# A two-layer hybrid decoder trunk on one core: six column sums per layer, each as two streamed passes over a rounded part and its rest

## The reference

```python
def rms_norm(x, g, eps=NORM_EPS):
    y = x * lax.rsqrt(jnp.mean(x * x, axis=-1, keepdims=True) + eps)
    return y * g

h = rms_norm(x, norm_g);  u = h @ w_in                                  # sum 0: over x
q = rms_norm(c_q, q_a_norm) @ w_q_b;  kv = rms_norm(c_kv, kv_a_norm) @ w_kv_b   # sums 1, 2
h = causal_depthwise_conv(a * sigmoid(g)); h = silu(layer_norm(h)); o = h @ w_pw  # sums 3, 4
y = rms_norm(y * silu(z), norm_g)                                       # sum 5: scan norm
x = x + concat([o_mla, o_conv, o_ssd]) @ w_out
```

## Time and profile before

| | |
|---|---|
| median of 3 runs | 1535.0 us (1534.81 to 1535.12) |
| profiled execution, its own time | 1534.9 us |
| its span, first to last instruction | 1533.1 us |
| TensorE (PE) busy | 1524.4 us, 99% |
| TensorE weight load (PEld) busy | 1225.4 us, 80% |
| VectorE (DVE) busy | 1007.6 us, 66% |
| ScalarE (ACT) busy | 683.0 us, 45% |
| GpSimd (POOL) busy | 43.5 us, 3% |
| granted TensorE clock, mean | 1.000 |

### The profile page before, as it was taken

The page is one execution under the profiler, slowest core; times in us unless marked ns, Lnnn a source line. Parts: engine busy times, 40 slices in busy tenths (PEclk is TensorE's granted clock), DMA queues, the critical chain, the costliest instruction groups (busy, mean ns, idle before and its releaser), DMA issues.

```text
span 1533.1 us, 18419 instructions
## 1 busy us (share of the span) xinstructions
PE 1524.4 (99%) x7086; PEld 1225.4 (80%) x7086; DVE 1007.6 (66%) x1497; ACT 683.0 (45%) x1013; POOL 43.5 (3%) x84
## 2 busy tenths in 40 slices
PE   8999999999999999999999999999999999999999
PEld 7887777877888888888887877778878888788887
DVE  7544675989999877443455456658999987663221
ACT  7445543334456645221244455543444566551111
POOL 0000000000000000110000000000000000001010
PEclk9999999999999999999999999999999999999999
DMA  6332223222233223544432232222223333235442
GB/s 228 109 91 71 96 69 96 69 69 73 90 110 107 90 83 110 168 146 143 144 103 79 83 97 83 82 76 77 69 69 103 99 118 99 77 110 165 138 151 83
DMA packets 44839, 158.13 MB, mean 103 GB/s; under 512 B 5552, under 2 KB 5840, under 8 KB 44752
## 3 DMA queue, kind: packets, MB, share of 16 engines
q1 hardware_dynamic: 38448, 134.36, 27.0%
q0 software_dynamic: 6304, 22.60, 5.2%
HBM read 148.50 MB, written 8.44 MB: 102 GB/s over the span
## 4 chain that ended last, share of the span: by engine, by line
PE 92%; DVE 5%; ACT 1%; issue 1%; DMA 0%; SPq 0%; DVEq 0%; ACTq 0%
PE acc L529 20%; PE acc L531 19%; PE acc L530 19%; PE S L534 5%; PE S L529 4%; PE S L530 4%; PE S L531 4%; PE T L531 4%; PE T L530 4%; PE T L529 4%; PE M L534 1%; PE O L534 1%; DVE wlo L1076 1%; PE T L534 1%; PE T L697 1%
## 5 line engine op out<-in xcount | busy, mean ns | idle before, releaser
L529 PE MATMUL acc<-hhi,whi 128*128 128x512 f32 (+1 forms) x1440 | 573.8, 398 | 2.9 <-DVE wlo L1161 1.1
L1076 DVE TENSOR_TENSOR wlo<-stage,whi 128x1024 fp32r<-128x1024 f32 (+2 forms) x251 | 299.3, 1197 | 412.9 <-ACT whi L793 409.8
L531 PE MATMUL acc<-hhi,wlo 128*128 128x512 f32 (+1 forms) x1440 | 561.7, 390 | 0.0
L530 PE MATMUL acc<-hlo,whi 128*128 128x512 f32 (+1 forms) x1440 | 560.8, 389 | 0.0
L793 ACT ACTIVATE whi<-stage 128x1024 fp32r<-128x1024 f32 (+2 forms) x251 | 259.2, 1036 | 516.9 <-PE acc L531 263.5
L529 PEld LDWEIGHTS acc<-hhi,whi 128*128 128x128 f32 (+1 forms) x1440 | 269.1, 187 | 64.2 <-issue 5.5
L531 PEld LDWEIGHTS acc<-hhi,wlo 128*128 128x128 f32 (+1 forms) x1440 | 268.9, 187 | 59.3
L530 PEld LDWEIGHTS acc<-hlo,whi 128*128 128x128 f32 (+1 forms) x1440 | 269.3, 187 | 57.8 <-issue 2.9
L1131 DVE SCALAR_TENSOR_TENSOR cacc<-glu,pv,cacc 128x512 f32<-128x512 f32 x240 | 168.8, 748 | 4.0
L781 ACT ACT_TABLE_LOAD x65 | 83.4, 1283 | 1.9 <-PEq L1618 0.7
L529 PE MATMUL S<-hhi,whi 128*128 128x512 f32 x192 | 75.6, 394 | 1.0 <-DVE wlo L1076 1.0
(11 more groups left out here) (241 smaller groups left out, 1568.3 us busy)
## 6 DMA issues: line engine op xcount, KB each, us to landing
stage<-weights SPq DMA_DIRECT2D x235, 512.0 KB, 3.4
y_features<-xg POOLq DMA_DIRECT2D x30, 256.0 KB, 4.2
acsb<-acs_rows POOLq DMA_DIRECT2D x16, 384.0 KB, 4.2
xr<-x_features POOLq DMA_DIRECT2D x16, 256.0 KB, 4.1
xr<-y_features POOLq DMA_DIRECT2D x16, 256.0 KB, 4.1
xg<-x_features SPq DMA_DIRECT2D x7, 512.0 KB, 7.9
stage<-weights SPq DMA_DIRECT2D x10, 256.0 KB, 2.7
stage<-weights SPq DMA_DIRECT2D x4, 384.0 KB, 3.1
```

Source lines behind the costliest of these rows:

```text
L529: nc.tensor.matmul(out, a, c, start=start, stop=False)
L530: nc.tensor.matmul(out, a, d, start=False, stop=False)
L531: return nc.tensor.matmul(out, b, c, start=False, stop=stop)
L1076: nc.vector.tensor_tensor(wlo[u % RING][:, 0:w], stage[u % STAGE][:, 0:w], whi[u % RING][:, 0:w].bitcast(F32), ALU.subtract).then_inc(lo_d ...
```

## The change

Each of the six inputs is split as the weights are. ScalarE copies the sum's input into a float32r tile (`sum_hi_of`), VectorE subtracts that from the input into a second one (`sum_lo_of`), and TensorE multiplies the ones matrix, read as float32r, with the first and then with the second into one bank. TensorE waits for `sum_lo` in place of the earlier signals. The tiles lie over buffers that are there already; SUM_HI and SUM_LO list them. Where each half stands in the lists: sums 0, 1, 2 in the steps rx, cq_sum, ckv_sum themselves; sums 3 and 4 in ln_sum and ln_square, two units ahead of the product; sum 5 in the step of tile 38, half 1. The four small products of ckv_sum stay as they are.

```diff
+        SUM_HI = [in_rcq, in_rckv, in_sqkp, in_rcq, in_rcq, in_sqkp]
+        SUM_LO = [in_sqx, in_sqc, in_kr2, in_sqkp, in_sqkp, in_kr2]
+        ones_r = ones[:, :].bitcast(F32R)
...
TensorE
-                def total(signal, parts, bank):
-                    last = None
-                    for i, part in enumerate(parts):
-                        last = full(bank[:, :], ones[:, :], part, i == 0, i == len(parts) - 1)
-                    last.then_inc(signal.sem, 1)
+                def total(i, bank):
+                    pe.wait_ge(sum_lo.sem, sum_lo.at(layer, i + 1))
+                    full(bank[:, :], ones_r, SUM_HI[i][:, :], True, False)
+                    return full(bank[:, :], ones_r, SUM_LO[i][:, :], False, True)
...
                     elif name == "rx":
                         pe.wait_ge(const_loaded.sem, 16)
-                        pe.wait_ge(sqx_ready.sem, sqx_ready.at(layer, 0))
-                        total(rx_sum, [sqx], M)
+                        total(0, M).then_inc(rx_sum.sem, 1)
                     elif name == "cq_sum":
                         pe.wait_ge(rx_ready.sem, rx_ready.at(layer, 1))
-                        pe.wait_ge(lat_sq.sem, lat_sq.at(layer, 4))
-                        total(lat_sum, [sqc], M)
+                        total(1, M).then_inc(lat_sum.sem, 1)
                     elif name == "ckv_sum":
                         pe.wait_ge(lat_r.sem, lat_r.at(layer, 1))
-                        pe.wait_ge(lat_sq.sem, lat_sq.at(layer, 6))
-                        full(M[:, :], ones[:, :], sqkv)
+                        total(2, M)
...                      (ln_mean, ln_var and ssd_sum likewise: total(3, M), total(4, M), total(5, T[1]))
ScalarE
+                def sum_hi_of(i, total):
+                    nc.scalar.activation(SUM_HI[i][:, :], total, ACT.Copy).then_inc(sum_hi.sem, 1)
...
+                            if (kind, i) == ("z", 5):
+                                act.wait_ge(ssd_sq.sem, ssd_sq.at(layer, 1))
+                                sum_hi_of(5, sqz[:, :])
...
                     elif name == "rx":
+                        act.wait_ge(sqx_ready.sem, sqx_ready.at(layer, 0))
+                        sum_hi_of(0, sqx)
                         act.wait_ge(rx_sum.sem, rx_sum.at(layer, 1))
                         rsqrt(rx_ready, rx[:, :], M[:, :], D_MODEL, 0)
...
                     elif name == "cq_sum":
+                        act.wait_ge(lat_sq.sem, lat_sq.at(layer, 4))
+                        sum_hi_of(1, sqc)
...
                     elif name == "ckv_sum":
+                        act.wait_ge(lat_sq.sem, lat_sq.at(layer, 6))
+                        sum_hi_of(2, sqkv)
...
+                    elif name == "ln_sum":
+                        act.wait_ge(conv_sum_in.sem, conv_sum_in.at(layer, 1))
+                        sum_hi_of(3, csum[:, :])
+                    elif name == "ln_square":
+                        act.wait_ge(conv_sum_in.sem, conv_sum_in.at(layer, 2))
+                        sum_hi_of(4, csum[:, :])
VectorE
+                def sum_lo_of(i, total):
+                    dve.wait_ge(sum_hi.sem, sum_hi.at(layer, i + 1))
+                    nc.vector.tensor_tensor(SUM_LO[i][:, :], total, SUM_HI[i][:, :].bitcast(F32),
+                                            ALU.subtract).then_inc(sum_lo.sem, 1)
...
                     elif name == "rx":
+                        sum_lo_of(0, sqx)
                         for j in range(3):
                             latent(j)
+                    elif name == "cq_sum":
+                        sum_lo_of(1, sqc)
+                    elif name == "ckv_sum":
+                        sum_lo_of(2, sqkv)
...                      (sum_lo_of(3) ends ln_sum, sum_lo_of(4) ends ln_square, sum_lo_of(5) ends gate z 5)
```

More of the change, by code:

```diff
@@ L255, in hybrid_kernel @@
         rx = sb("rx", [P, SEQ])
-        rcq = sb("rcq", [P, SEQ])
-        rckv = sb("rckv", [P, SEQ])
+        at_rcq, at_rckv = region(4 * SEQ), region(4 * SEQ)
+        rcq = sb("rcq", [P, SEQ], F32, at_rcq)
+        rckv = sb("rckv", [P, SEQ], F32, at_rckv)
         temp = sb("temp", [P, SEQ])
@@ L289, in hybrid_kernel @@
         xw = sb("xw", [P, GH * SSD_P], F32, m4 + 10240)
-        kr2 = sb("kr2", [P, SEQ])
-        sqkp = sb("sqkp", [P, SEQ])
+        at_kr2, at_sqkp = region(4 * SEQ), region(4 * SEQ)
+        kr2 = sb("kr2", [P, SEQ], F32, at_kr2)
+        sqkp = sb("sqkp", [P, SEQ], F32, at_sqkp)
         e0 = region(8192)
         sqh = sb("sqh", [P, 4, SEQ], F32, e0)
+        in_rcq, in_rckv, in_kr2, in_sqkp, in_sqx, in_sqc = (
+            sb(f"sum_{n}", [P, SEQ], F32R, at) for n, at in (("rcq", at_rcq), ("rckv", at_rckv), ("kr2", at_kr2),
+                                                            ("sqkp", at_sqkp), ("sqx", e0 + 6144), ("sqc", e0)))
+        SUM_HI = [in_rcq, in_rckv, in_sqkp, in_rcq, in_rcq, in_sqkp]
+        SUM_LO = [in_sqx, in_sqc, in_kr2, in_sqkp, in_sqkp, in_kr2]
+        ones_r = ones[:, :].bitcast(F32R)
         sqc, sqkv, kd, sqx = sqh[:, 0, :], sqh[:, 1, :], sqh[:, 2, :], sqh[:, 3, :]
@@ L406, in hybrid_kernel @@
         conv_r = sig("conv_r", 1)
+        sum_hi = sig("sum_hi", 6)
+        sum_lo = sig("sum_lo", 6)
         ln_centred = sig("ln_centred", 4)
@@ L730, in _ @@
                     elif name == "ln_mean":
-                        pe.wait_ge(conv_sum_in.sem, conv_sum_in.at(layer, 1))
                         pe.wait_ge(proj_taken.sem, proj_taken.at(layer, 15))
-                        total(conv_sum, [csum[:, :]], M)
+                        total(3, M).then_inc(conv_sum.sem, 1)
                     elif name == "ln_var":
-                        pe.wait_ge(conv_sum_in.sem, conv_sum_in.at(layer, 2))
-                        total(conv_sum, [csum[:, :]], M)
+                        total(4, M).then_inc(conv_sum.sem, 1)
                     elif name == "pw":
@@ L749, in _ @@
                     elif name == "ssd_sum":
-                        pe.wait_ge(ssd_sq.sem, ssd_sq.at(layer, 1))
                         pe.wait_ge(ssd_in.sem, ssd_in.at(layer, 8))
-                        total(ssd_sum, [sqz[:, :]], T[1])
+                        total(5, T[1]).then_inc(ssd_sum.sem, 1)
                     elif name == "out2":
@@ L1309, in _ @@
                                 tt(ssd_sq if i == 5 else None, sqz[:, :], sqz[:, :], temp[:, :], ALU.add)
+                            if i == 5:
+                                sum_lo_of(5, sqz[:, :])
                         elif kind == "ua":
@@ L1444, in _ @@
                         tt(conv_sum_in, csum[:, :], csum[:, :], cacc[:, 3, :], ALU.add)
+                        sum_lo_of(3, csum[:, :])
                     elif name == "ln_mean":
@@ L1454, in _ @@
                         tt(conv_sum_in, csum[:, :], csum[:, :], ln_y[:, 3, :], ALU.add)
+                        sum_lo_of(4, csum[:, :])
                     elif name == "ln_apply":
```

## The result

The changed kernel takes 1559.8 us (median of four runs, 1558.2 to 1561.0) against 1535.0: 1.0161 times as long, 95% interval 1.0149 to 1.0173. That is 24.8 us more. The forecast was 1549, its range ended at 1556.

What follows compares the result with a forecast made beforehand. TensorE's own instruction list was taken to bound the kernel: 1534.9 + 16.3 (waits at sums 0 to 2) - 2.4 (sums 3 to 5) = 1548.8, forecast 1549 us; range 1546.5 to 1556.

Steps and rivals of the forecast that it cites:

- Six waits: TensorE waits for late halves at sums 0, 1 and 2 in both layers: +16.3 us in two layers.
- The clock: TensorE's pace after idling about 3.1 us at sums 0 and 2: no slowdown assumed, 0 us added.
- this rival: The clock falls in the six stalls at sums 0 to 2, 1.8 us each: 1560 us at most, chance 0.11.
- the gain of sums 3 to 5: Streaming at sums 3, 4 and 5 in two layers, halves in time: 6 sums at -0.40, -2.4 us.
- the room can only grow: At sums 3 to 5 halves have 1.4 us or more to spare; TensorE arrives 8.2 us later, so no wait.
- The faster rival: Halves ready when TensorE arrives, copy running before the unit's split; all twelve sums gain 0.40 us: 1530 us, chance 0.04.

Runs made afterwards that it cites:

- the filled kernel: The changed kernel with 14, 11 and 14 additional streamed products on TensorE ahead of its wait at sums 0, 1 and 2: 1550.7 us.
- sums 0 to 2 alone: The changed kernel with only sums 0, 1 and 2 streamed, sums 3, 4 and 5 float32 as before the change: 1559.0 us.

## Why the prediction was right and wrong

**Right: what bounds, where it waits, and how long.** TensorE's list was the time. Six waits came where the list puts them, 3.2, 2.5 and 3.2 us long, and none at sums 3 to 5. With the clock steady they cost 2.94, 2.23 and 3.00 us a layer, where the prediction had 2.94, 2.22 and 3.01. The step that carried the forecast, that the copy stands behind a `split` which waits for the very unit ahead of the sum, was shown twice: moving the halves ahead of it took the loss away, and that wait alone, in the kernel before, brought a loss of the same size.

**Wrong: the step "The clock", "I take nothing, as after the 1.1 us".** I carried the full pace behind 1.1 us of idleness over to 3.1 us, three times as long, although the only long idleness in the trace, the one ahead of the kernel's start, was followed by the lower level. The runs: 1559.8 with the idleness, 1550.7 with the same waits filled, so 9.1 us, and the sign that the prediction named, matmuls 0.43 us apart behind a stall, was there. The forecast priced this rival at 6 x 1.8 = 10.8 and 1560 in all. (The 3.6 us behind that price were read a little short: the last record of 421 ns starts at 4.68 us and ends its turn at 4.89, which makes 3.8.) That 1560 was measured is partly luck: the clock fell five times and not six in the profiled execution, for about 3.4 or 6.7 us and not for 3.6, which came to 9.1 in place of 10.8, and the gain of sums 3 to 5 was 1.2 us too high. The size was near all the same; it was the chance of 0.11 and the upper end of the range at 1556 that were wrong. The rival with a price near the right one and a row of its own should have been in the range at least.

By the rule named in the prediction, from the Trainium skill ("TensorE: Matmul & The Clock Gate", section "The HAM clock gate"), that an idle TensorE is throttled to half rate and has to be busy for a while to get the full one back, the traces agree for five of the six waits, with 0.43 in place of 0.23 us a matmul; at the sixth, sum 1 of layer 0, the clock stayed at 1.00.

**Mis-sized: the gain of sums 3 to 5.** The term was -2.4 us. Alone they gave 1.1. The pass pair takes 0.46 us as forecast (sum 4 here: 543.21 to 543.68), but "the room can only grow" looked at the sums' own waits only. The halves also move ScalarE's gate and the norm's chain, and TensorE waits for that chain 25 us later, 0.51 us in place of 0.22; with the small delays around it the stage takes back 0.58 us a layer. In the kernel before, this wait of 0.2 us was the sign that the stage had no room left.

**The sum again.** 1535.0 + 16.3 (waits, as forecast and as read in the filled kernel) - 1.1 (sums 3 to 5, as measured alone) = 1550.2, where the filled kernel stands at 1550.7. The clock's 9.1 us bring it to 1559.3, against 1559.8; since they are the difference between these two kernels, this second step is no test of its own.

**The faster rival** (1530) decided at the point it named, the place of the copy. With the copy there it gave 1533.9: at two sums the halves still come late and TensorE waits 0.4 and 0.2 us for them, which costs 0.2 us a layer at the one and leaves no gain at the other, and the layer norm stage took its share. Four sums chosen by where there is room gave 1532.0.

## What to carry to other kernels

Ahead of a wait that is added to the bounding engine, read what stands in line before the helpers' work on their engines: here an instruction that waits for that same engine. On TensorE price each new idle stretch beyond those that the trace shows to be harmless twice, once for the wait and once for the pace behind it, and keep the second in the range. A gain on the bounding engine counts only up to the next place where it already waits a little for another.

## What the runs showed of the hardware

The clock's fall depends on more than the length of one idle stretch. In the profiled executions it fell at waits of 3.2 us 8 times out of 8 (in the whole change and in sums 0 to 2 alone), at 2.3 to 2.6 us 10 out of 14, at 1.76 us 0 of 2, at 1.5 us 2 of 4, at 1.0 us 0 of 2. A fall took about 3.4 or 6.7 us at the lower level, and of two waits of one length in one run one can have it and the other not; what picks them stayed open. Kernels with such waits scatter by 0.9 to 5.0 us from run to run, those without by 0.3 to 1.6.
